# Differential attention with three slots of score banks and its map combination shared by VectorE and GpSimd

## The chip, the cores and the metric

The kernel runs on one core of one Trainium2 chip. The metric is the device time of one execution in microseconds. Engines are named as in the profile: PE is TensorE, DVE VectorE, ACT ScalarE, POOL GpSimd, SP SyncE. PSUM has eight banks of 512 float32 columns per partition; here all eight form one tensor `ps`.

## What is computed

A hybrid transformer of 2 layers on 512 tokens of width 1024, then a second block of 4 layers on the 512 latent tokens and 256 context tokens, with three kinds of mixers in turn. The change lies in the third layer of the second block, the only one of kind 2 (`mixer_c`), differential attention with 8 head pairs, each with two score maps of head width 64:

```python
def diff_attention(q, k, v, lam):
    scale = HEAD_DIM ** -0.5
    def block(j, qb):
        logits = jnp.einsum("bqhmd,bkhmd->bhmqk", qb, k).astype(jnp.float32) * scale
        p = jax.nn.softmax(logits, axis=-1)
        a = (p[:, :, 0] - lam * p[:, :, 1]).astype(v.dtype)
        return jnp.einsum("bhqk,bkhd->bqhd", a, v)
    return map_query_blocks(block, q)
...
o = finish(diff_attention(q, jnp.concatenate([kc, k], axis=1), jnp.concatenate([vc, v], axis=1), lam), s)
oc = finish(diff_attention(qc, kc, vc, lam), n_ctx) if need_ctx else None
```

Latent queries see all 768 keys, context queries the 256 context keys.

## The kernel before

The stage is the first one of `difference_attention` (lines 1283 to 1428). Its work is a list of 48 units in groups. A unit is one tile of 128 queries of one pair, with both of its maps. `second_block` makes the groups: first eight groups (one per pair) of four latent units, 768 keys each, then eight groups of two context units, 256 keys each. Queries and keys of a group are split into a high and a low float32r part; the next group's parts are made during a group by ACT (`q_high`, `k_high`) and POOL (`q_low_plain` L1117, `k_low` L1127).

Each engine runs its own loop over the units, in a fixed order with semaphores between them. For one unit:

- PE makes the scores of both maps (L1145), latent ones in four banks, two for each map; the next unit's scores go into the same four banks, so PE waits for both exponentials of this one (context units alternate between two pairs of banks).
- DVE takes each row's maximum of both maps from PSUM (L1407), ACT the exponentials with their row sums (L1362), a pair of instructions for each map; ring of three units in `prob`.
- DVE computes the reciprocals of the sums (L1397) and a weight per row (L1399), then combines both maps over all 768 columns in one instruction (L1419): map 1 times weight plus map 0.
- PE transposes the combined map two units later, six blocks (L1331), into banks 4 or 5 and bank 6; ACT copies the first four blocks to SBUF (L1370), DVE the other two, the tail (L1414). PE multiplies with the values three units later (L1343) into bank 7, ACT scales that into `prj` (L1354).
- Once per group, for the norm of the outputs: POOL clamps (L1306), ACT squares twice (L1386, L1389), DVE reduces to `near` and `far` (L1426).

A second stage (lines 1436 to 1493) scales the outputs. Two lines set what PE waits for before the scores:

```python
        return 2 * x - 2 if x and self.double(x) and self.double(x - 1) else 2 * x
...
                            pe.wait_ge(exped, max(1, W.exps_ahead(x)))
```

## Time and profile before

| | |
|---|---|
| three runs | 3370.6, 3384.76, 3385.7 us, median 3384.76 |
| the profiled execution | 3373.4 us, its span 3371.6 us |
| busy over the span | PE 3180.3 us (94%), DVE 1503.1 (45%), ACT 1340.1 (40%), POOL 1154.5 (34%) |
| mean granted TensorE clock | 0.98 |
| the stage of the change | from 2747.7 to 2931.3 us of the span |

Busy time is the time in which an engine has an instruction under way. The profiled execution's own time is what it reports as a run; its span is from its first to its last instruction. The other stages have no instruction that the change touches.

### The profile page before, as it was taken

How to read it: one execution, taken by the hardware profiler on the slowest of the kernel's cores; microseconds unless marked ns; L12 is line 12 of the kernel's file. 1: busy time of each engine (PE TensorE's matmuls, PEld its weight loads, DVE VectorE, ACT ScalarE, POOL GpSimd, SP SyncE). 2: the span in 40 equal slices, each digit the busy share in tenths (PEclk: the TensorE clock that was granted, in tenths of full speed). 3: DMA queues.
4: the chain of work that ended last, by engine and by line, in shares of the span. 5: the costliest groups of instructions: out<-in, count | busy, mean ns of one | idle time of the engine just before them, and what ended most of it. 6: DMA issues, size and time to landing. Idle time of an engine off the chain costs nothing. (4 is left out here: it accounts for less than half of the span.)

```text
span 3371.6 us, 52216 instructions
## 1 busy us (share of the span) xinstructions
PE 3180.3 (94%) x20854; PEld 2602.3 (77%) x20854; DVE 1503.1 (45%) x2671; ACT 1340.1 (40%) x2452; POOL 1154.5 (34%) x640
## 2 busy tenths in 40 slices
PE   7989999999989999989999999999999988799998
PEld 6857788877667888878787888777888767588787
DVE  4963444118744343131376310267323348833473
ACT  4353333223433333242366313267223237733463
POOL 4531444445314444434201322242234422226202
PEclk9999999999999999989999999999999999899999
DMA  4345222223452222222000111110112200013102
GB/s 148 114 158 187 82 100 94 98 84 120 157 192 77 100 94 97 100 91 88 26 2 18 56 60 63 55 44 15 57 62 88 76 19 1 4 54 103 48 2 76
DMA packets 81815, 262.19 MB, mean 78 GB/s; under 512 B 11936, under 2 KB 13344, under 8 KB 81568
## 3 DMA queue, kind: packets, MB, share of 16 engines
q1 hardware_dynamic: 81568, 258.79, 22.7%
q8 instruction: 169, 2.77, 0.3%
q14 instruction: 78, 0.64, 0.1%
HBM read 239.34 MB, written 2.10 MB: 72 GB/s over the span
## 5 line engine op out<-in xcount | busy, mean ns | idle before, releaser
L175 PE MATMUL ps<-hs,head 128*128 128x512 f32 x4176 | 868.3, 365 | 18.5 <-PEq L95 5.6
L175 PE MATMUL ps<-hs,WS 128*128 128x512 f32 x4176 | 861.3, 364 | 7.6 <-POOL WS L156 7.6
L175 PEld LDWEIGHTS ps<-hs,head 128*128 128x128 f32 x4176 | 713.0, 189 | 167.1 <-issue 19.1
L175 PEld LDWEIGHTS ps<-hs,WS 128*128 128x128 f32 x4176 | 713.3, 189 | 144.2 <-POOL WS L156 9.7
L156 POOL TENSOR_TENSOR WS<-W,WS 128x1024 fp32r<-128x1024 f32 x168 | 406.3, 2418 | 618.0 <-ACT WS L148 618.0
L156 POOL TENSOR_TENSOR head<-W,head 128x1024 fp32r<-128x1024 f32 x165 | 398.3, 2414 | 616.7 <-ACT head L148 616.5
L148 ACT CAST WS<-W 128x1024 fp32r<-128x1024 f32 x168 | 176.2, 1049 | 350.8 <-PE ps L175 324.2
L1630 ACT ACTIVATE prob<-ps,low 128x768 f32<-128x768 f32 (+4 forms) x320 | 223.4, 700 | 181.4 <-DVE low L1702 178.7
L1702 DVE TENSOR_REDUCE low<-ps 128x1 f32<-128x768 f32 (+4 forms) x320 | 216.5, 702 | 94.8 <-PE ps L1145 90.4
L148 ACT CAST head<-W 128x1024 fp32r<-128x1024 f32 x165 | 172.7, 1047 | 198.8 <-PE ps L175 198.6
L1145 PE MATMUL ps<-kk,qq 64*128 64x256 f32 (+3 forms) x2064 | 214.2, 334 | 38.3 <-ACT prob L1362 24.2
L1145 PEld LDWEIGHTS ps<-kk,qq 64*128 64x128 f32 x2064 | 158.0, 185 | 104.3 <-issue 50.7
L1117 POOL TENSOR_TENSOR qq<-prj,qq 128x512 fp32r<-128x512 f32 (+1 forms) x54 | 55.8, 1033 | 415.6 <-ACT qq L1110 406.0
L2072 DVE TENSOR_TENSOR glu<-cg,glu 128x512 fp32r<-128x512 f32 x44 | 81.0, 1840 | 258.1 <-ACT glu L2046 258.1
L1597 PE MATMUL ps<-const,prob 128*128 128x128 f32 x1312 | 182.9, 280 | 6.7 <-ACT probT L1638 3.3
L1612 PE MATMUL ps<-probT,vtok 128*64 128x128 f32 x2624 | 178.6, 279 | 2.4 <-DVE prj L1686 2.4
L1597 PEld LDWEIGHTS ps<-const,prob 128*128 128x128 f32 x1312 | 140.3, 141 | 38.4 <-ACT prob L1630 11.4
L2354 ACT ACTIVATE prj<-ps,par 128x768 f32<-128x768 f32 (+1 forms) x52 | 45.3, 871 | 306.1 <-PE ps L175 306.1
L1612 PEld LDWEIGHTS ps<-probT,vtok 128*64 128x64 f32 x2624 | 140.0, 136 | 27.6 <-issue 27.1
L1638 ACT COPY probT<-ps 128x512 f32<-128x512 f32 (+3 forms) x272 | 139.7, 541 | 1.7 <-PE ps L1597 1.4
L2104 DVE TENSOR_TENSOR xT<-xT,ps 128x512 f32<-128x512 f32 x32 | 22.0, 687 | 253.9 <-PE ps L175 253.9
L175 PE MATMUL ps<-head,hs 128*128 128x512 f32 (+2 forms) x624 | 120.4, 350 | 9.5 <-DVE hs L375 5.4
(290 smaller groups left out, 3925.4 us busy)
## 6 DMA issues: line engine op xcount, KB each, us to landing
W<-in_stream_dram SPq DMA_DIRECT2D x432, 512.0 KB, 3.5
swap<-prj SPq DMA_DIRECT2D x168, 64.0 KB, 2.1
band<-in_bias_band_dram SPq DMA_DIRECT2D x8, 512.0 KB, 3.5
prj<-prj SPq DMA_DIRECT2D x64, 64.0 KB, 2.9
xT<-in_x_dram SPq DMA_DIRECT2D x4, 512.0 KB, 8.3
W<-in_stream_dram SPq DMA_DIRECT2D x1, 2048.0 KB, 13.6
xT<-turned SPq DMA_DIRECT2D x8, 256.0 KB, 6.5
out_dram<-xT SPq DMA_DIRECT2D x8, 256.0 KB, 2.7
```

The costliest lines, as they stand in the source:

```text
L148: nc.scalar.copy(WS[j % 2][:, 0, :], M.W[:, (pos + j) % RING, :]).then_inc(high, 1)
L156: nc.gpsimd.tensor_tensor(WS[j % 2][:, 1, :], M.W[:, (pos + j) % RING, :], WS[j % 2][:, 0, :], ALU.subtract).then_inc(split, 1)
L175: last = pe.matmul(out, a(i), b(j), start=start and n == 0, stop=stop and n == 2)
L1117: return self.nc.gpsimd.tensor_tensor(self.q_part(s, 1, cols), self.queries(t, cols), self.q_part(s, 0, cols), ALU.subtract)
L1145: last = pe.matmul(out(hd)[:, sc:sc + c], self.qq[s][half(hd), i, q0:q0 + P], self.kk[s_keys][half(hd), j, kc:kc + c], start=n == 0, stop= ...
L1597: last = pe.transpose(turn_at(y, hd, j), prob[:, (2 * y + hd) % 4, sc:sc + P], M.const[:, C_ID:C_ID + P])
L1612: pe.matmul(summed_at(hd), M.vtok[:, kb, v_col(p) + 64 * hd:v_col(p) + 64 * hd + 64], probT[:, (2 * y + hd) % 4, j, :], start=j == 0, stop ...
L1630: nc.scalar.activation(prob[:, u % 4, c0:c0 + n], W.scores(M, x, hd)[:, c0:c0 + n], ACT.Exp, bias=low[:, u:u + 1], accum_out=total[:, u:u ...
L1638: nc.scalar.copy(probT[:, u % 4, 0:n, :], M.ps[:, 4 + 2 * hd, 0:n * P].rearrange("p (x n) -> p x n", n=P)).then_inc(turn_copied, 1)
L1702: nc.vector.tensor_reduce(low[:, u:u + 1], W.scores(M, x, hd)[:, c0:c0 + n], AX_X, ALU.max, negate=True).then_inc(maxed, 1)
L2072: nc.vector.tensor_tensor(glu[:, 1, f - 2, :], g[:, f % 2, :], glu[:, 0, f - 2, :], ALU.subtract).then_inc(glu_split, 1)
L2354: nc.scalar.activation(M.prj[:, t, 0:n], flat(bank(t), n), ACT.Copy, scale=gain(t)).then_inc(evicted, 1)
```

## The change

Score banks: the maps of all units go in turn through three slots of two banks (0 to 5), so the scores of unit x wait for the exponentials 0 to 2x-2, not for both of unit x-1. `prob` becomes a ring of four units. All transposes use bank 6, the first four blocks (the front) and then the last two (the back); they come three units after the scores, the product with the values four units after. DVE copies the front to SBUF, ACT the back. DVE combines the first 384 columns of a latent unit (all 256 of a context unit); POOL combines the last 384 in two instructions, a multiplication by the weight and an addition. DVE takes the maximum of map 1 after reciprocal, weight and front copy. A group is now one pair with four latent and two context units, so query and key parts are made eight times, for 768 queries, and clamp, squares and reductions are 768 wide. The scratch for dynamic DMAs is set to 1024 bytes, which frees SBUF.

```diff
@@ -1259,47 +1259,58 @@
...
-    ring, n_keys = 3, operands.n_keys
+    ring, n_keys, front = 4, operands.n_keys, 3 * P
...
-        clamped, scaled = sbuf(nc, mem, "clamped", [P, 2, S]), sbuf(nc, mem, "scaled", [P, S])
+        clamped, scaled = sbuf(nc, mem, "clamped", [P, 2, N]), sbuf(nc, mem, "scaled", [P, N])
...
-        turn_at = lambda x, j: (M.ps[:, 4 + x % 2, j * P:j * P + P] if j < 4 else M.ps[:, 6, (j - 4) * P:(j - 3) * P])
+        backs = lambda n: sum(not W.small(x) for x in range(n))
+        turns = lambda n: n + backs(n)
+        parts = lambda x: [W.columns(x)[i:i + 4] for i in range(0, W.size(x) // P, 4)]
+        turned_parts = lambda x, i: M.ps[:, 6, 0:len(parts(x)[i]) * P].rearrange("p (x n) -> p x n", n=P)
...
-        scores = lambda x, hd: W.scores(M, x, hd)[:, W.first(x):W.first(x) + W.size(x)]
...
+        def banks(x, hd):
+            b = 2 * ((2 * x + hd) % 3)
+            return M.ps[:, b:b + 2, :].rearrange("p b n -> p (b n)")
+
+        first = lambda x: 0 if W.small(x) else W.first(x)
+        scores = lambda x, hd: banks(x, hd)[:, first(x):first(x) + W.size(x)]
...
             @block.gpsimd
             def _(pool):
-                for y in range(X + 4):
+                for y in range(X + 3):
                     if y < X:
-                        g = works[y][0] + 1
-                        n, last = y - W.start[g - 1], len(groups[g - 1][3]) - 1
+                        pool.wait_ge(weight_known, y + 1)
+                        if not W.small(y):
+                            x = unit(y, 1)[:, front:]
+                            nc.gpsimd.tensor_tensor(x, x, weight[:, y:y + 1].broadcast_to([P, n_keys - front]), ALU.mult
+                                                    ).then_inc(back_weighted, 1)
+                            pool.wait_ge(back_weighted, backs(y + 1))
+                            nc.gpsimd.tensor_tensor(x, x, unit(y, 0)[:, front:], ALU.add).then_inc(back_combined, 1)
+                        g, n = works[y][0] + 1, y - W.start[works[y][0]]
                         if g < len(groups):
                             p, q_cols, k_cols, _ = groups[g]
-                            if n == min(1, last - 1):
+                            if n == 1:
                                 pool.wait_ge(queries_high, g)
-                                if y:
-                                    pool.wait_ge(weight_known, y)
                                 operands.q_low_plain(g % 2, p, q_cols).then_inc(queries_low, 1)
-                            if n == min(2, last - 1):
+                            if n == 2:
                                 pool.wait_ge(keys_high, g)
-                                if y:
-                                    pool.wait_ge(weight_known, y)
                                 operands.k_low(g % 2, p, k_cols).then_inc(keys_low, 1)
-                    if y - 3 in ends:
-                        g = ends.index(y - 3)
+                    if y - 2 in ends:
+                        g = ends.index(y - 2)
                         pool.wait_ge(raw_copied, ends[g])
                         if g >= 2:
                             pool.wait_ge(reduced, 2 * (g - 1))
@@ -1308,76 +1319,75 @@
 
             @block.tensor
-                for x in range(X + 3):
+                def turn(y, i):
+                    if y + i:
+                        pe.wait_ge(front_copied, y + i)
+                    if backs(y) and not i:
+                        pe.wait_ge(back_copied, backs(y))
+                    for j, sc in enumerate(parts(y)[i]):
+                        last = pe.transpose(M.ps[:, 6, j * P:j * P + P], prob[:, (2 * y + 1) % (2 * ring), sc:sc + P],
+                                            M.const[:, C_ID:C_ID + P])
+                    last.then_inc(turned, 1)
+
+                for x in range(X + 4):
...
                         if x:
-                            pe.wait_ge(exped, max(1, W.exps_ahead(x)))
-                        operands.scores(pe, lambda hd: W.scores(M, x, hd), g % 2, g % 2, m * P // 2, keys
-                                        ).then_inc(scored, 1)
+                            pe.wait_ge(exped, 2 * x - 1)
+                        operands.scores(pe, lambda hd: banks(x, hd), g % 2, g % 2, m * P // 2,
+                                        [(keys[0][0], 0, CTX)] if W.small(x) else keys).then_inc(scored, 1)
                         if x < 3:
                             keep_running(pe, M, 4, 7)
+                    if 3 <= x < X + 3:
+                        pe.wait_ge(front_combined, x - 2)
+                        if backs(x - 2):
+                            pe.wait_ge(back_combined, backs(x - 2))
+                        turn(x - 3, 0)
+                    if x >= 4:
+                        y = x - 4
-                        pe.wait_ge(turn_copied, y + 1)
-                        if W.tail(y):
-                            pe.wait_ge(tail_copied, tails(y + 1))
+                        pe.wait_ge(front_copied, y + 1)
+                        pe.wait_ge(back_copied, backs(y + 1))
...
+                    if 3 <= x < X + 3 and not W.small(x - 3):
+                        turn(x - 3, 1)
...
                             if x >= ring:
-                                act.wait_ge(turned, x - ring + 1)
+                                act.wait_ge(turned, turns(x - ring + 1))
                             nc.scalar.activation(unit(x, hd), scores(x, hd), ACT.Exp, bias=low[:, u:u + 1],
                                                  accum_out=total[:, u:u + 1]).then_inc(exped, 1)
-                    if 2 <= x < X + 2:
-                        y = x - 2
-                        n = min(4, W.size(y) // P)
-                        act.wait_ge(turned, y + 1)
-                        if y >= 2:
-                            act.wait_ge(weighted, y - 1)
-                        nc.scalar.copy(probT[:, y % 2, 0:n, :], M.ps[:, 4 + y % 2, 0:n * P].rearrange(
-                            "p (x n) -> p x n", n=P)).then_inc(turn_copied, 1)
+                    if 3 <= x < X + 3 and not W.small(x - 3):
+                        y = x - 3
+                        act.wait_ge(turned, turns(y + 1))
+                        nc.scalar.copy(probT[:, y % 2, 4:, :], turned_parts(y, 1)).then_inc(back_copied, 1)
...
             @block.vector
             def _(dve):
+                def largest(x, hd):
+                    u = 2 * x + hd
+                    nc.vector.tensor_reduce(low[:, u:u + 1], scores(x, hd), AX_X, ALU.max, negate=True
+                                            ).then_inc(maxed, 1)
+
                 for x in range(X + 8):
+                    if x < X:
+                        dve.wait_ge(scored, x + 1)
+                        largest(x, 0)
...
-                    for hd in range(2):
-                        if x < X:
-                            u = 2 * x + hd
-                            if hd == 0:
-                                dve.wait_ge(scored, x + 1)
-                            nc.vector.tensor_reduce(low[:, u:u + 1], scores(x, hd), AX_X, ALU.max, negate=True
-                                                    ).then_inc(maxed, 1)
-                    if 2 <= x < X + 2 and W.tail(x - 2):
-                        y = x - 2
-                        dve.wait_ge(turned, y + 1)
+                    if 3 <= x < X + 3:
+                        y = x - 3
+                        dve.wait_ge(turned, turns(y) + 1)
                         if y >= 2:
                             dve.wait_ge(weighted, y - 1)
-                        nc.vector.tensor_copy(probT[:, y % 2, 4:4 + W.tail(y), :], M.ps[:, 6, 0:W.tail(y) * P].rearrange(
-                            "p (x n) -> p x n", n=P)).then_inc(tail_copied, 1)
+                        nc.vector.tensor_copy(probT[:, y % 2, 0:len(parts(y)[0]), :], turned_parts(y, 0)
+                                              ).then_inc(front_copied, 1)
+                    if x < X:
+                        largest(x, 1)
                     if 1 <= x <= X:
                         y = x - 1
+                        n = CTX if W.small(y) else front
                         dve.wait_ge(weight_known, y + 1)
-                        nc.vector.scalar_tensor_tensor(unit(y, 1), unit(y, 1), weight[:, y:y + 1], unit(y, 0), ALU.mult,
-                                                       ALU.add).then_inc(combined, 1)
+                        nc.vector.scalar_tensor_tensor(unit(y, 1)[:, 0:n], unit(y, 1)[:, 0:n], weight[:, y:y + 1],
+                                                       unit(y, 0)[:, 0:n], ALU.mult, ALU.add).then_inc(front_combined, 1)
...
@@ -2509,14 +2523,17 @@
                     tiles = ([(2 * m + 1, ((m * P, 0, NEAR), context_keys), (0, 0, NEAR)) for m in range(QT - 1)] +
                              [("edges", ((0, 0, P), (S - P, P, P), context_keys), (0, 0, NEAR))])
                 groups = [(p, (0, S), (0, N), tiles) for p in range(PAIRS2)]
-                if go_on:
+                if kind == 2:
+                    tiles += [context(m) for m in range(QT, NT)]
+                    groups = [(p, (0, N), (0, N), tiles) for p in range(PAIRS2)]
+                elif go_on:
                     groups += [(p, (S, N), (S, N), [context(m) for m in range(QT, NT)]) for p in range(PAIRS2)]
...
-                    first_rows(nc, M, FirstRows(operands, (0, S), (0, N)))
+                    first_rows(nc, M, FirstRows(operands, groups[0][1], (0, N)))
...
-    nc = bacc.Bacc("TRN2", target_bir_lowering=False, num_devices=1)
+    nc = bacc.Bacc("TRN2", target_bir_lowering=False, num_devices=1, dynamic_dma_scratch_size=1024)
```

DVE in the steady part of the latent units, all rows of one unit, before:

```order
L1399 SCALAR_TENSOR_TENSOR weight<-inv,small,total 128x1
L1407 TENSOR_REDUCE low<-ps 128x1 x2
L1414 COPY probT<-ps 128x256
L1419 SCALAR_TENSOR_TENSOR prob<-prob,weight 128x768
L1397 RECIPROCAL inv<-total 128x2
```

and with the change:

```order
L1405 TENSOR_REDUCE low<-ps 128x1
L1415 RECIPROCAL inv<-total 128x2
L1417 SCALAR_TENSOR_TENSOR weight<-inv,small,total 128x1
L1425 COPY probT<-ps 128x512
L1405 TENSOR_REDUCE low<-ps 128x1
L1433 SCALAR_TENSOR_TENSOR prob<-prob,weight 128x384
```

The second maximum moved behind the weight and the copy from PSUM, which is now the front of 512 columns, and the combine is half as wide.

POOL in one group of the change, from its second latent unit (`prob` is the pair of maps, `qq` and `kk` are the low parts of the next group, `clamped` the outputs of the last one):

```order
L1299 TENSOR_TENSOR prob<-prob,weight 128x384
L1302 TENSOR_TENSOR prob<-prob 128x384
L1117 TENSOR_TENSOR qq<-prj,qq 128x768
L1299 TENSOR_TENSOR prob<-prob,weight 128x384
L1302 TENSOR_TENSOR prob<-prob 128x384
L1127 TENSOR_TENSOR kk<-prj,kk 128x768
L1317 TENSOR_SCALAR clamped<-prj 128x768
L1299 TENSOR_TENSOR prob<-prob,weight 128x384
L1302 TENSOR_TENSOR prob<-prob 128x384
```

Before, POOL had in this stage three rows a group, L1117, L1127 and L1306. Two rows per latent unit were added ahead of them.

PE for one latent unit, before:

```order
L1145 MATMUL ps<-kk,qq 128x512 x6
L1145 MATMUL ps<-kk,qq 128x256 x6
L1331 MATMUL ps<-const,prob 128x128 x6
L1343 MATMUL ps<-vtok,probT 128x128 x6
```

and with the change:

```order
L1145 MATMUL ps<-kk,qq 128x512 x6
L1145 MATMUL ps<-kk,qq 128x256 x6
L1328 MATMUL ps<-const,prob 128x128 x4
L1357 MATMUL ps<-vtok,probT 128x128 x6
L1328 MATMUL ps<-const,prob 128x128 x2
```

The last two transposes moved behind the product and stand ahead of the next unit's scores.

## Rows read from the trace of the kernel before

**Rows 1.** Timeline, the marks: start us, length us, engine, operation [idle before]
```profile
2747.76 1.31 PE L1145 MATMUL ps<-kk,qq 64*128 64x512 f32 x12 [1.74 <-PEq L95]
...
2885.53 0.62 PE L1145 MATMUL ps<-kk,qq 64*128 64x256 f32 x6 [1.03 <-ACT prob L1362]
...
2920.77 0.61 PE L1145 MATMUL ps<-kk,qq 64*128 64x256 f32 x6
...
2930.93 0.41 DVE L1426 TENSOR_REDUCE far<-scaled 128x2 f32<-128x256 f32 x1
```

**Rows 2.** Stretches: us; PE, PEld, DVE, ACT, POOL busy; clock, DMA
```profile
2747.70:2885.50 137.80, 112.21 (x936) 96.33 (x937) 113.89 (x198) 98.37 (x215) 27.45 (x23) 1.00 0.00 1
...
2899.00:2925.00 26.00, 20.54 (x132) 15.32 (x132) 21.52 (x67) 23.37 (x89) 9.75 (x16) 0.87 0.00 1
```

**Rows 3.** Timeline, one latent unit on PE, DVE and ACT
```profile
2769.26 1.31 PE L1145 MATMUL ps<-kk,qq 64*128 64x512 f32 x12 [0.82 <-ACT prob L1362]
...
2770.50 0.64 PEld L1331 LDWEIGHTS ps<-const,prob 128*128 128x128 f32 x6
...
2770.62 1.82 DVE L1407 TENSOR_REDUCE low<-ps 128x1 f32<-128x768 f32 x2 [0.88 <-PE ps L1145]
2771.11 1.42 PEld L1343 LDWEIGHTS ps<-vtok,probT 128*128 128x128 f32 x12
...
2771.62 0.90 ACT L1362 ACTIVATE prob<-ps,low 128x768 f32<-128x768 f32 x1 [1.66 <-DVE low L1407]
2772.36 0.42 DVE L1414 COPY probT<-ps 128x256 f32<-128x256 f32 x1
...
2772.51 0.89 ACT L1362 ACTIVATE prob<-ps,low 128x768 f32<-128x768 f32 x1
2772.69 1.01 DVE L1419 SCALAR_TENSOR_TENSOR prob<-prob,weight 128x768 f32<-128x768 f32 x1
...
2773.54 1.33 PE L1145 MATMUL ps<-kk,qq 64*128 64x512 f32 x12 [0.82 <-ACT prob L1362]
2773.62 0.16 DVE L1397 RECIPROCAL inv<-total 128x2 f32<-128x2 f32 x1
2773.81 0.22 DVE L1399 SCALAR_TENSOR_TENSOR weight<-inv,small,total 128x1 f32<-128x1 f32 x1
```

**Rows 4.** Groups by line and form: count | busy us, mean ns | idle before
```profile
L1718 DVE COPY probT<-ps 128x512 f32<-128x512 f32 x64 | 43.6, 681 | 4.6 <-PE ps L1597 4.6
...
L1407 DVE TENSOR_REDUCE low<-ps 128x1 f32<-128x256 f32 x32 | 12.1, 419 | 4.5 <-PE ps L1145 4.2
...
L1419 DVE SCALAR_TENSOR_TENSOR prob<-prob,weight 128x256 f32<-128x256 f32 x16 | 8.1, 509 | 0.0
...
L1127 POOL TENSOR_TENSOR kk<-prj,kk 128x768 fp32r<-128x768 f32 x20 | 36.4, 1821 | 54.5 <-ACT kk L1124 39.9 <-DVEq L92 14.6
...
L1306 POOL TENSOR_SCALAR clamped<-prj 128x512 f32<-128x512 f32 x8 | 5.2, 646 | 0.7
...
L1005 POOL TENSOR_TENSOR k_far<-k_far,prj 128x384 f32<-128x384 f32 x2 | 2.0, 998 | 0.0
L981 POOL TENSOR_TENSOR q_far<-prj 128x384 f32<-128x384 f32 x2 | 1.7, 870 | 0.0
```

**Rows 5.** Timeline, three places where DVE and POOL work at once
```profile
390.98 2.40 POOL L156 TENSOR_TENSOR head<-W,head 128x1024 fp32r<-128x1024 f32 x1 [3.48 <-ACT head L148]
391.97 1.95 DVE L2072 TENSOR_TENSOR glu<-cg,glu 128x512 fp32r<-128x512 f32 x1 [8.12 <-ACT glu L2046]
...
2779.06 1.81 POOL L1127 TENSOR_TENSOR kk<-prj,kk 128x768 fp32r<-128x768 f32 x1 [3.21 <-ACT kk L1124]
...
2779.20 1.82 DVE L1407 TENSOR_REDUCE low<-ps 128x1 f32<-128x768 f32 x2 [0.88 <-PE ps L1145]
...
2881.86 0.74 POOL L1127 TENSOR_TENSOR kk<-prj,kk 128x256 fp32r<-128x256 f32 x1 [3.53 <-DVE near L1426]
2881.91 0.69 DVE L1399 SCALAR_TENSOR_TENSOR weight<-inv,small,total 128x1 f32<-128x1 f32 x1
```

More of the change, by code:

```diff
@@ L1261, in difference_attention @@
     X, works, groups = W.X, W.works, W.groups
-    tails = lambda n: sum(W.tail(x) > 0 for x in range(n))
     ends = W.start[1:]
-    ring, n_keys = 3, operands.n_keys
+    ring, n_keys, front = 4, operands.n_keys, 3 * P
     width = lambda g: len(groups[g][3]) * P
@@ L1349, in _ @@
                 for x in range(X + 6):
-                    if 4 <= x < X + 4:
-                        p, m = works[x - 4][1:3]
-                        act.wait_ge(weighted, x - 3)
-                        act.wait_ge(inverted, x - 3)
-                        nc.scalar.activation(M.prj[:, p, m * P // 2:m * P // 2 + P], summed, ACT.Copy,
-                                             scale=inv[:, 2 * (x - 4):2 * (x - 4) + 1]).then_inc(raw_copied, 1)
                     if x < X:
```

36 lines of the change are left out of this document (14 added, 22 removed).

## The prediction

> **What bounds the kernel now.** The page comes first: over the whole span PE is busy 94% of the time, so most of this kernel is matmul and is not touched. The change lies in one stage, so that stage is cut out of the trace. Its first scores start at 2747.76, the first context unit's at 2885.53, the last unit's at 2920.77, and its last reduction ends at 2931.34, 183.6 us after the start [rows 1]. So 32 latent units take 137.8 us (4.31 each) and 15 steps of context units 35.2 us (2.35 each); one pair costs 4 x 4.31 + 2 x 2.35 = 21.9 us. In the latent stretch no engine is full: DVE 114 of 138 us, PE 112, ACT 98, POOL 27 [rows 2]. What sets the period is a loop, and one unit in order of time shows it [rows 3]: the scores start at 2769.26; DVE gets them after 1.36 us and takes two row maxima; the first exponential starts 1.00 later, the second 0.89 after that, it is done 1.03 later, and the next scores start at 2773.54. That is 4.28. PE waited 0.81 us for ACT. DVE's own work in it, from start to start, is 1.74 (two maxima) + 0.33 (tail copy) + 0.93 (combine) + 0.33 (reciprocal and weight) = 3.33 us.
>
> **What the change does to that loop.** With three score slots, scores of unit x+1 need only the first exponential of unit x, so the second maximum and the second exponential leave the loop: 1.36 + 1.00 + 1.03 = 3.4 us would be left. But the loop is then no longer the limit; the queues of DVE and POOL are. I walked the 48 units through the new order of the four engines rules: an instruction starts when its engine is free and 0.05 us after what it waits for, and it holds its engine for the start-to-start time of the rows. On PE these are 1.24 for latent scores, 0.11 per transposed block and 1.42 for a product of six blocks; on ACT 0.88 per exponential [rows 3]. A pair is four latent units a to d and two context units e and f.
>
> DVE's own work for a pair, by start-to-start times: maxima 4 x 1.74 + 2 x 0.68 = 8.32 (a 256-column one takes 0.42 [rows 4], of which 0.08 overlaps the next, as with the long ones); reciprocals and weights 6 x 0.33 = 1.98; front copies from PSUM, 4 of 512 columns and 2 of 256, 4 x 0.61 + 2 x 0.33 = 3.10 (0.68 and 0.42 long [rows 3, 4]); combines: 768 columns take 1.01 and 256 take 0.51, so 384 take 0.61, and 4 x 0.53 + 2 x 0.40 = 2.92; near and far, now 768 columns, 2 x 0.87 = 1.74 (as a maximum of that width). Sum 18.1. The old order's DVE work for the same six units was nearly the same (4 x 3.33 + 2 x 1.41, and near and far of 1.9, so 18.0): halving the combine saves 4 x 0.40, the longer front copy gives back 4 x 0.28, and the context units' copies, which were ACT's, come on top.
>
> POOL's work rises steeply. An in-place two-input operation of 384 columns takes 1.00, one with a repeated column 0.87 [rows 4]: 1.87 per latent unit, 0.05 between them for the semaphore, plus per pair two 768-column low parts of 1.82 and a clamp (0.65 at 512 columns, so 0.9). Some 12 us per pair, below DVE's; as a queue it has room.
>
> **Does POOL's work lie beside DVE's for nothing? The trace says no.** A DVE product with two SBUF inputs, 512 columns, starts at 391.97 while POOL runs from 390.98 to 393.38. It ends at 393.92, which is 0.54 after POOL's end: it stood still until then [rows 5]. A one-column weight instruction, 0.22 long elsewhere [rows 3], starts at 2881.91, 0.05 after POOL's k_low, and takes 0.69, to POOL's end at 2882.60 [rows 5]. Two maxima, which read PSUM, take 1.82 beside a POOL operation and 1.82 without one [rows 3, 5]. So combine and weight are held by a POOL operation under way, maxima are not, and copies from PSUM I take to be like maxima, since both read one input and that from PSUM. The Trainium skill says in "SBUF — State Buffer", section "Who interferes with whom", that a VectorE instruction with at most one SBUF input does not contend; by this the trace's maxima agree, and the front copies would be free as I take them.
>
> The holds in the walk (microseconds from a's first maximum): weight of a at 5.01; POOL multiplies from 5.28 to 6.14 and adds from 6.19 to 7.19. DVE meanwhile copies and takes the second maximum and is at the combine of a at 6.35: held to 7.19, then 0.40 of columns, a loss of 0.71. Unit b repeats it, 0.71. POOL then does q_low until 13.86, so the weight of c (DVE there at 13.16) loses 0.56, and its combine 0.35. k_low until 17.98 holds the weight of d 1.09, clamp and multiplication its combine 0.68, the addition of d the weight of e 0.28. Together 4.4 us. DVE waits 1.0 more for scores, where PE sits behind the front copy. A pair: 18.1 + 4.4 + 1.0 = **23.4 us against 21.9**.
>
> No row shows the two POOL operations themselves. Bounds: 0.62 each from below (one input over 512 columns takes 0.65 [rows 4]), 1.25 from above (the 1.00 with half a further input for the weight). The walk gives 22.4 and 24.6 us a pair at these ends. I take the rows of the same width. As the holds come from few examples, their ends are nothing (rival A) and the full 4.4.
>
> The Trainium skill, "GPSIMD Engine Reference", section "4.1 Engine selection", sends elementwise multiplications to VectorE, with GpSimd about 2 times slower for two inputs. By that rule each half-width operation would be 2 x 0.61 = 1.2 us, an estimate from the page; the walk would come to 24.3 us a pair, and the stage would be 7 us longer still.
>
> **The sum.** Walk: first two pairs 21.7 and 22.1 (the pipe fills, nothing behind the first scores), five pairs at 23.4, the last up to its sixth scores 19.6: 180.4. The drain is longer than before: it is one unit deeper, and clamp, two squares and two reductions of the last pair are 768 wide in a row: 15.0 instead of 10.6. Stage 195.4. The same walk over the old order gives 180.6 where the trace has 183.6, so I scale by 1.016: 198.5, **+14.9**. Ahead of it the first high part of the queries (ACT) grows by 256 columns, and its low part (DVE) now ends beside POOL's k_low: +0.3, at about 1 ns a column as in the combine. On PE all work stays, and its share of the time falls. It had the full 2.4 GHz (granted 1.00) in the latent stretch and 0.87 of it on average among context units, where PE was waiting more [rows 2]; I add 1 us. Total +16. DMAs: none added; all are issued by SP, so the smaller scratch costs nothing, and no DMA runs in this stage (share 0.00 [rows 2]) that could be late.
>
> Against the profiled execution's own 3373.4 (span 3371.6) that is 3389. The median of the three runs, 3384.8, stands 11 above the profiled one, and against it I forecast **3401**. A measurement of this kernel tells from no change about 0.5%, 17 us; the forecast lies just at that line.
>
> **The rivals.**
> A, the holds are absorbed. In the walk with no hold DVE waits 3.3 us per pair for scores, PE being behind copies: the pair is 21.35 and the stage 184.4, scaled. Holds of 4.4 that fell wholly into such waits or that turned round (DVE first at the port, POOL waiting, which has room) would leave this. For: POOL's slack; the margins at a and b are only 0.16 us. Against: weight and combine stand in DVE's own queue before the next maximum. Decided by whether the combine reaches the port before the addition. It gives +1: 3386, not slower.
> B, real overlap: the extra score slot keeps DVE fed, neither holds nor waits bind, and a pair costs little over DVE's 18.1, say 19.4; with the longer drain that is 20 us less, 3365. Against: PE is in order, and the second turn stands ahead of the next scores, behind the front copy. It decides if the front copy is done before PE has finished its products.
> C, the clock. PE's own work by the walk's times is 15.6 of 23.4 us per pair. If the granted clock stays near 0.87 [rows 2], that work grows by 2.3 us per pair, at worst all on the path, 18 us; the walk with PE's operations 15% longer gives 6 us more. So 3407, at most 3419. For: context units now come every pair, and PE waits up to 2 us there. Against: 0.87 came only after a run of small units.
>
> **How the numbers follow.** Forecast (3393 to 3411) 0.50, A 0.22, B 0.10, C 0.18. Faster by over 0.5% (under 3368) is B and the rim of A: 0.12. Slower by over 0.5% (over 3401.7) is C and half of the forecast: 0.45. The rest, 0.43, is within. The range takes in the bounds of the POOL prices (22.4 to 24.6 per pair: -8 and +10), A, and the lower half of C: 3374 to 3416.
>
> **What would show it.** In the changed profile: L1405 of 768 columns starts again 23.4 us later from pair to pair; L1433 of 384 columns with a mean near 1.1 rather than 0.61; L1417 with single ones of 0.5 to 1.2; L1299 and L1302 at 0.86 and 1.00; L1405's wait for PE small, because DVE is nearly full. Wrong if L1433 stays near 0.6 (A), if pairs take 20 us (B), if the clock of the stage is under 0.95 (C), or if L1425 is held by POOL too, which the walk leaves out.

## The result, and the profile after

The changed kernel takes 3404.31 us (median of 5 runs, 3400.48 to 3408.2), the kernel before 3380.59 (5 runs, 3370.6 to 3385.7): a ratio of 1.007, 95% interval 1.0054 to 1.0085. That is 23.7 us slower. The forecast was 3401 with a range of 3374 to 3416, so the time is met. Its closeness is partly luck: I had added 16 us to a median of 3384.76, the fuller median is 4 lower, and on the old one the same +23.7 would have given 3408.5, still inside the range but 7.5 over the forecast instead of 3.3. The 8 us missing from my +16 are the lesson of this case.

The page of the kernel after, its first lines:

```profile
span 3402.5 us, 52186 instructions
...
PE 3202.4 (94%) x20854; PEld 2617.9 (77%) x20854; DVE 1522.2 (45%) x2671; ACT 1329.2 (39%) x2404; POOL 1211.8 (36%) x680
```

The marks of the stage in its timeline, answering to [rows 1] (start us, length us, engine, operation):

```profile
2754.49 1.31 PE L1145 MATMUL ps<-kk,qq 64*128 64x512 f32 x12 [2.00 <-PEq L95]
...
2947.01 0.64 PE L1145 MATMUL ps<-kk,qq 64*128 64x256 f32 x6
...
2961.41 0.94 DVE L1440 TENSOR_REDUCE far<-scaled 128x6 f32<-128x768 f32 x1
```

From first scores to last reduction the stage takes 207.9 us against 183.6: +24.3, the whole difference of the medians. Behind it both traces take the same (440.15 and 440.26 us). Ahead of it this one is 6.7 later, but that start lies between 2743.7 and 2758.8 over all the profiles below, whatever the edit, so 6.4 of it is scatter; the wider first rows are the 0.3 forecast (query high part 0.84 instead of 0.63).

Stretches after, answering to [rows 2]: the whole stage, then the second pair and three of the steady ones (us; PE, PEld, DVE, ACT, POOL busy; clock, DMA):

```profile
2754.49:2962.35 207.86, 163.57 (x1176) 134.08 (x1176) 167.65 (x304) 126.11 (x303) 97.56 (x86) 0.89 0.00 1
...
2778.67:2801.08 22.41, 17.68 (x145) 14.24 (x144) 19.48 (x37) 13.91 (x37) 12.88 (x11) 1.00 0.01 1
...
2801.08:2826.29 25.21, 21.16 (x145) 17.41 (x145) 21.55 (x39) 15.89 (x39) 12.70 (x11) 0.80 0.00 1
...
2826.29:2851.16 24.87, 20.26 (x145) 16.94 (x144) 20.91 (x39) 15.78 (x39) 12.71 (x11) 0.86 0.00 1
...
2851.16:2875.41 24.25, 18.73 (x145) 15.48 (x144) 21.29 (x39) 15.75 (x39) 12.71 (x11) 0.93 0.00 1
```

Two things stand there. A steady pair takes 24.25 to 25.6 us, the walk gave 23.4. And the clock is not the 1.00 of the old latent stretch: it was 0.97 over the stage before and is 0.89 now. Only the second pair runs at 1.00, and it takes 22.4, where the walk gave 22.1.

Groups of the stage by line and form, answering to [rows 4] (count | busy us, mean ns | idle before), and from the view of single lines the spread of each (ns min/median/max):

```profile
L1405 DVE TENSOR_REDUCE low<-ps 128x1 f32<-128x768 f32 x64 | 60.6, 949 | 20.0 <-PE ps L1145 20.0
...
L1433 DVE SCALAR_TENSOR_TENSOR prob<-prob,weight 128x384 f32<-128x384 f32 x32 | 32.2, 1006 | 0.0
...
L1405 DVE TENSOR_REDUCE low<-ps 128x1 f32<-128x256 f32 x32 | 13.3, 416 | 13.6 <-PE ps L1145 13.6
```

```profile
L1433 DVE SCALAR_TENSOR_TENSOR prob<-prob,weight x48: 470/610/1392, 2762.7 to 2951.7; 128x384 f32<-128x384 f32 x32, 128x256 f32<-128x256 f32 x16
...
L1417 DVE SCALAR_TENSOR_TENSOR weight<-inv,small,total x48: 219/220/1247, 2761.7 to 2950.2; 128x1 f32<-128x1 f32 x48
...
L1425 DVE COPY probT<-ps x48: 417/678/693, 2769.3 to 2955.2; 128x512 f32<-128x512 f32 x32, 128x256 f32<-128x256 f32 x16
...
L1299 POOL TENSOR_TENSOR prob<-prob,weight x32: 825/826/1197, 2762.0 to 2944.4; 128x384 f32<-128x384 f32 x32
...
L1302 POOL TENSOR_TENSOR prob<-prob x32: 992/1009/1327, 2762.9 to 2945.3; 128x384 f32<-128x384 f32 x32
```

The combine of 384 columns takes 1.01 us in the mean where an unheld one takes 0.61, a weight up to 1.25 where it needs 0.22, and the copy from PSUM is never held. POOL's two operations take 0.83 and 1.01 in the median (0.89 and 1.05 in the mean, as some are held themselves), the prices taken from rows of the same width. DVE waits 33.6 us for scores, in a stage where I had called it nearly full.

How a hold looks, and what the clock does, in the timeline of the third pair (start us, length us):

```profile
2818.24 2.13 POOL L1127 TENSOR_TENSOR kk<-prj,kk 128x768 fp32r<-128x768 f32 x1
...
2819.16 1.23 DVE L1417 SCALAR_TENSOR_TENSOR weight<-inv,small,total 128x1 f32<-128x1 f32 x1
...
2820.07 2.77 PE L1357 MATMUL ps<-vtok,probT 128*128 128x128 f32 x12
...
2821.26 0.61 DVE L1433 SCALAR_TENSOR_TENSOR prob<-prob,weight 128x384 f32<-128x384 f32 x1
2821.36 1.20 POOL L1299 TENSOR_TENSOR prob<-prob,weight 128x384 f32<-128x384 f32 x1
...
2824.25 0.42 DVE L1405 TENSOR_REDUCE low<-ps 128x1 f32<-128x256 f32 x1 [2.38 <-PE ps L1145]
...
2824.64 1.50 PE L1357 MATMUL ps<-vtok,probT 128*128 128x128 f32 x12
...
2833.93 1.02 POOL L1302 TENSOR_TENSOR prob<-prob 128x384 f32<-128x384 f32 x1
2833.97 1.39 DVE L1433 SCALAR_TENSOR_TENSOR prob<-prob,weight 128x384 f32<-128x384 f32 x1
```

The one-column weight starts at 2819.16 and ends at 2820.39, with POOL's low part (2820.37). The combine of 2833.97, 0.04 behind POOL's addition, ends 0.41 after it. At 2821.26 the combine comes first: it takes its 0.61, and POOL's multiplication is the one held (1.20 instead of 0.83). And the product at 2820.07 takes 2.77 us where the next, at 2824.64, takes 1.50 for the same matmuls: half the clock for most of it, and DVE then waits 2.38 us for the scores queued behind it.

### The profile page after: what moved, and what is told of

It reads as the page before. It is cut to its first block and busy times, and to the rows that moved or that the text cites. A ratio compares the mean times of both kernels' runs of the same rounds, so it can differ in the third digit from the quotient of the medians.

```text
span 3402.5 us, 52186 instructions
## 1 busy us (share of the span) xinstructions
PE 3202.4 (94%) x20854; PEld 2617.9 (77%) x20854; DVE 1522.2 (45%) x2671; ACT 1329.2 (39%) x2404; POOL 1211.8 (36%) x680
## 3 DMA queue, kind: packets, MB, share of 16 engines
q8 instruction: 169, 2.77, 0.3%
## 5 line engine op out<-in xcount | busy, mean ns | idle before, releaser
L175 PEld LDWEIGHTS ps<-hs,head 128*128 128x128 f32 x4176 | 715.5, 190 | 165.8 <-issue 19.4
L175 PEld LDWEIGHTS ps<-hs,WS 128*128 128x128 f32 x4176 | 712.9, 189 | 144.6 <-POOL WS L156 10.5
L1644 ACT ACTIVATE prob<-ps,low 128x768 f32<-128x768 f32 (+4 forms) x320 | 223.2, 699 | 183.4 <-DVE low L1716 180.8
L1117 POOL TENSOR_TENSOR qq<-prj,qq 128x512 fp32r<-128x512 f32 (+2 forms) x46 | 55.5, 1207 | 311.4 <-ACT qq L1110 310.9
## 6 DMA issues: line engine op xcount, KB each, us to landing
W<-in_stream_dram SPq DMA_DIRECT2D x1, 2048.0 KB, 13.6
```

Source lines behind the costliest of these rows:

```text
L175: last = pe.matmul(out, a(i), b(j), start=start and n == 0, stop=stop and n == 2)
L1117: return self.nc.gpsimd.tensor_tensor(self.q_part(s, 1, cols), self.queries(t, cols), self.q_part(s, 0, cols), ALU.subtract)
L1644: nc.scalar.activation(prob[:, u % 4, c0:c0 + n], W.scores(M, x, hd)[:, c0:c0 + n], ACT.Exp, bias=low[:, u:u + 1], accum_out=total[:, u:u ...
```

## The experiments

All are measured against the kernel before on the same chip (3376.0, 3378.3 and 3377.8 us in the three sets). The first number of each is its median, and the ratio is the one on record with its interval. The ratio is not the quotient of the two medians and differs from it by up to 0.2%, or 6 us. A stage is read from one profile each.

### The scratch alone, and the grouping alone

```diff
-    nc = bacc.Bacc("TRN2", target_bir_lowering=False, num_devices=1)
+    nc = bacc.Bacc("TRN2", target_bir_lowering=False, num_devices=1, dynamic_dma_scratch_size=1024)
```

> The kernel before with only the scratch for dynamic DMAs set to 1024 bytes. In the changed kernel's profile the stage starts 6.7 us later in the span than before, though only 0.3 of that was expected from the wider first rows. Theory that this is scatter between executions, as the three runs before differ by 15 us: no difference, ratio 1.000 within 0.002. Rival, the smaller scratch slows the weight stream: about +6 us, ratio 1.002.

3375.3 us, ratio 0.9994 (0.9983 to 1.0004), stage 183.4: the scratch costs nothing, and it can be kept in the others.

The kernel before with the scratch and with groups of four latent and two context units (768-wide `clamped` and `scaled` with them), nothing else:

```diff
-                if go_on:
+                if kind == 2:
+                    tiles += [context(m) for m in range(QT, NT)]
+                    groups = [(p, (0, N), (0, N), tiles) for p in range(PAIRS2)]
+                elif go_on:
```

> The kernel before with the change's groups (one pair, four latent and two context units; 768-wide parts, clamp, squares, reductions) and its scratch, nothing else. By the walk, a context unit inside a group costs 2.6 us instead of 2.3 on average, and the last drain is wider: stage 191 against 183.6, +8 us, if the clock stays as before. If units of both kinds side by side lower TensorE's clock: +12 to +20. Rival, the grouping only saves work (half as many low and high parts) and the loss is all from POOL and the slots: -2 to 0 us.

3391.5 us, ratio 1.0042 (1.0028 to 1.0055), +14 by the ratio, with the old slots and no new work on POOL. The stage takes 194.6, +11. Two of its pairs, the third and the seventh, the same instructions in each:

```profile
2804.10:2826.58 22.48, 16.79 (x146) 14.24 (x145) 18.50 (x36) 16.61 (x41) 4.45 (x3) 1.00 0.00 1
...
2895.40:2918.65 23.25, 18.34 (x145) 15.57 (x144) 18.50 (x36) 16.61 (x41) 4.45 (x3) 0.93 0.00 1
```

Latent steps are 4.28 as before. A context step is 2.69 or 2.70 each time, where a long run of context units had pipelined to 2.35: 16 of them make 5.4 us. The clock falls to 0.93 in five of the first seven pairs (never in the old latent stretch [rows 2]), with six single latent steps of 4.5 to 5.25, 4.0 us together over the usual 4.28. The drain behind the last unit's scores takes 13.3 us instead of 10.6. Grouping is thus dear by itself.

The other way round, the changed kernel with the groups of before (and the places of the high and low parts that go with them):

> The changed kernel with the groups of before (eight of four latent units, then eight of two context units); slots, order and the shared combination stay. Walk with POOL holding DVE: stage 199, as slow as the changed one, with 4.6 us per latent unit, since low parts still come every fourth unit. If the grouping (and the clock it costs) is what made it slow and the holds cost little: stage about 185 or less, +2 us over before.

3399.2 us, ratio 1.0059 (1.0038 to 1.008), stage 205.45, 6 over the walk's 199: almost nothing came back. The profile shows a wait that the old grouping brings with it (timeline ahead of the fifth group's first scores):

```profile
2820.31 0.83 POOL L1299 TENSOR_TENSOR prob<-prob,weight 128x384 f32<-128x384 f32 x1 [1.04 <-DVE weight L1421]
...
2821.22 0.99 POOL L1302 TENSOR_TENSOR prob<-prob 128x384 f32<-128x384 f32 x1
...
2822.17 2.12 POOL L1127 TENSOR_TENSOR kk<-prj,kk 128x768 fp32r<-128x768 f32 x1
...
2824.39 1.04 PE L1145 MATMUL ps<-kk,qq 64*128 64x512 f32 x6 [3.06 <-issue]
```

With four units a group the key low part is the last thing before the next group's scores, and it now stands behind multiplication and addition: every fourth step is 6.8 us, and PE stands still for 3. The profile names no releaser for that idle time ("issue"), but the scores start 0.10 us after the low part's end. The two context units in the new groups had covered that. So groups and POOL's queue are coupled, and undoing either alone shows little. The clock falls here with the old groups too: it is 0.93 over the latent units, where the kernel before had 1.00.

### What POOL's half costs

The changed kernel, DVE combining all 768 columns:

```diff
-    ring, n_keys, front = 4, operands.n_keys, 3 * P
+    ring, n_keys, front = 4, operands.n_keys, 6 * P
...
-                        if not W.small(y):
-                            x = unit(y, 1)[:, front:]
...
```

> The changed kernel with the whole combination on DVE (one instruction of 768 columns, 1.0 us) and none on POOL. DVE's own work per pair rises by 4 x 0.4 = 1.6 us, the holds by multiplication and addition (about 3 of 4.4 us) go. Walk: 22.7 to 23.1 us per pair, stage 193 to 198 before any loss of clock, so 2 to 5 us faster than the changed kernel. If DVE's load is the limit and holds are nothing: 3 x 1.6 to 8 x 1.6 us, 5 to 13 slower than the changed kernel. If only the clock matters: the same as the changed kernel.

3392.9 us, ratio 1.0031 (1.0018 to 1.0043), stage 202.4: 16.9 us over the kernel before by the medians and 10.5 by the ratio, where the whole change has 23.7, and 5.4 less in the stage: faster than with POOL's help. DVE does twice the columns and yet loses nothing by it, its combine taking 1.26 us for 768 columns (some still held by low parts) against 1.01 held for 384. Of the 5.4 us, 4.2 lie in the steps from the first to the second context unit, four of which take 3.99 us here and only one as little in the changed kernel; the section on the clock explains these.

POOL's two instructions left out, DVE keeping 384 columns (the last 384 stay uncombined):

> The changed kernel in which the last 384 columns of each latent unit's combination are left out: POOL does neither multiplication nor addition, those columns keep map 1's exponentials. DVE's work is unchanged. Theory of the holds: combines come back to 0.61 us but for those behind low parts and clamp; walk 22.0 us per pair or less, stage 186 to 194 against 207.9 in the changed kernel's profile, so 14 to 20 us faster than the changed kernel. Rival, the loss is the clock and PE's order: at most 3 us faster.

3391.6 us, ratio 1.0032 (1.0019 to 1.0044), stage 193.7, 14.2 less than the changed kernel. The combine still takes 0.86 us in the mean, since low parts now fall beside it. And in their place two memsets of nearly the same length on POOL, into a buffer of their own, with the same semaphores:

```diff
-                            x = unit(y, 1)[:, front:]
-                            nc.gpsimd.tensor_tensor(x, x, weight[:, y:y + 1].broadcast_to([P, n_keys - front]), ALU.mult
-                                                    ).then_inc(back_weighted, 1)
+                            if backs(y):
+                                pool.wait_ge(back_combined, backs(y))
+                            nc.gpsimd.memset(idle[:, 0:864], 0.0).then_inc(back_weighted, 1)
...
-                            nc.gpsimd.tensor_tensor(x, x, unit(y, 0)[:, front:], ALU.add).then_inc(back_combined, 1)
+                            nc.gpsimd.memset(idle[:, 0:1024], 0.0).then_inc(back_combined, 1)
```

> As the kernel with the last 384 columns left out, but POOL writes zeros to a buffer of its own (864 and 1024 columns of bfloat16) in place of multiplication and addition, with the same semaphores: POOL is as busy in its queue and PE waits for it, but it reads nothing. Theory that the loss is VectorE held while POOL reads SBUF: no holds, within 4 us of the kernel with the columns left out, combines of 0.61 us. Rival, the loss is that PE waits for a slow POOL queue: as slow as the changed kernel. If any POOL instruction holds DVE, also writes: combines of 1.0 us and as slow as the changed kernel.

3389.4 us, ratio 1.0039 (1.0023 to 1.0055). Its groups in the stage:

```profile
L1303 POOL MEMSET idle<- 128x1024 bf16 x32 | 30.4, 951 | 1.9
L1301 POOL MEMSET idle<- 128x864 bf16 x32 | 26.2, 817 | 88.9 <-DVE weight L1418 87.9
L1434 DVE SCALAR_TENSOR_TENSOR prob<-prob,weight 128x384 f32<-128x384 f32 x32 | 19.4, 607 | 0.0
L1418 DVE SCALAR_TENSOR_TENSOR weight<-inv,small,total 128x1 f32<-128x1 f32 x48 | 17.4, 362 | 1.7
```

POOL is nearly as long busy (88 us of the stage, 98 with the real work), it stands as long between weight and transposes, its memsets do write SBUF, and yet the combine takes 0.607 each time and the stage 194.9. So not the queue and not the writing costs the 13 us, but that POOL reads. (2.1 of the 13 lie in the steps from the first to the second context unit, where the clock falls less often.) The Trainium skill says in "SBUF — State Buffer", section "Who interferes with whom", that a VectorE instruction with two SBUF inputs contends with a GpSimd instruction that reads SBUF and not with one that only writes; these two runs agree (1.01 beside reading operations, 0.61 beside memsets). The weight's 0.36 is that of units held by operations which still read, the low parts above all (0.5 and 0.95 us).

### The clock

In the run without POOL's half the same pair appears at both clocks:

```profile
2821.41:2843.21 21.80, 17.48 (x146) 14.19 (x146) 19.10 (x39) 15.74 (x39) 4.46 (x3) 1.00 0.00 1
2843.21:2866.45 23.24, 18.91 (x145) 15.63 (x145) 19.05 (x38) 15.76 (x39) 4.46 (x3) 0.93 0.00 1
```

and its timeline shows where, transposes and product in the step of the first context unit, first at full clock, then not:

```profile
2838.35 0.63 PE L1322 MATMUL ps<-const,prob 128*128 128x128 f32 x4 [1.25 <-ACT probT L1369]
2838.82 1.50 PE L1349 MATMUL ps<-vtok,probT 128*128 128x128 f32 x12
...
2860.16 1.09 PE L1322 MATMUL ps<-const,prob 128*128 128x128 f32 x4 [1.25 <-ACT probT L1369]
2861.04 2.53 PE L1349 MATMUL ps<-vtok,probT 128*128 128x128 f32 x12
```

The step grows from 3.99 to 5.43 us, the pair from 21.80 to 23.24, by the same 1.44. One fall of the clock there costs 1.4 us, wholly on the path, since DVE and ACT wait for the scores behind that product. Both times PE had been idle 1.22, 1.05 and 1.25 us in turn just ahead, so these gaps alone don't decide whether the clock falls.

I then tried to hold the clock with idle transposes in the changed kernel:

```diff
+                    if 3 <= x < X and x - W.start[works[x][0]] in (2, 3, 4, 5):
+                        pe.wait_ge(exped, 2 * x)
+                        for _ in range(4):
+                            pe.matmul(M.ps[:, 2 * ((2 * x + 2) % 3), 0:P], M.const[:, C_ID:C_ID + P], M.const[:, 0:P],
+                                      start=True, stop=True)
```

> The changed kernel with four idle transposes of 128 columns (0.42 us at the full clock) on PE ahead of the back's transposes, in the last four steps of each pair, where PE waits for copies anyway; they write to the score bank that is free next. Nothing else of it changes. The stage's mean granted clock is 0.89 in the changed kernel against 0.97 before, and its step from e to f takes 5.2 to 5.9 us where the walk has 4.1. Theory that the 9 us over the forecast stage are the clock: the clock rises to 0.95 or more, the stage falls by 4 to 9 us. Rival, the long step is order, not clock: the stage grows by up to 32 x 0.42 = 13 us, or stays.

3410.6 us, ratio 1.0096 (1.0076 to 1.0115), stage 212.1, 4.2 longer where the theory had it 4 to 9 shorter. Two stretches of one pair's length, each from the scores of a second context unit to those of the next:

```profile
2799.05:2823.84 24.79, 21.05 (x178) 17.77 (x177) 21.28 (x38) 15.85 (x38) 12.69 (x12) 1.00 0.01 2
2823.84:2850.25 26.41, 22.69 (x177) 19.41 (x177) 21.28 (x38) 15.86 (x38) 13.99 (x13) 0.94 0.00 1
```

The clock rose (0.97 over the stage) and the step fell from 5.2 to 5.9 down to 4.88 in five pairs of eight, but the fillers (32.8 us of PE in all) put the time back: 24.79 for a pair at full clock, as much as an unfilled one at 0.86. As a remedy it fails: the stage grew, as the rival had it, though the clock rose. As a test it agrees that the long step is the clock (4.88 at 1.00, 6.3 to 6.5 in the three pairs where the clock fell all the same) and says nothing cleaner on its size, as the fillers also add a wait of PE for two exponentials.

### The order of the queues

The changed kernel with the old groups, POOL's low parts ahead of its half, and reciprocal and weight behind both maxima:

```diff
                             if n == min(1, last - 1):
                                 pool.wait_ge(queries_high, g)
+                                if y:
+                                    pool.wait_ge(weight_known, y)
...
+                        pool.wait_ge(weight_known, y + 1)
+                        if not W.small(y):
+                            x = unit(y, 1)[:, front:]
...
```

> The changed kernel with three things put differently: the groups of before; POOL makes the low parts ahead of multiplication and addition (the next group's scores waited 6.8 us every fourth unit for the keys' low part in the run with the old groups); DVE computes reciprocal and weight after both maxima, so that the combine follows the weight at once and starts before POOL's multiplication. Theory of the holds: the walk gives 174 to 179, scaled 177 to 182, 2 to 7 us faster than before. If holds were not the cause and the three slots themselves lose: as slow as the run with the old groups, 20 us over before.

3376.1 us, ratio 0.9993 (0.9982 to 1.0005), stage 182.2. The wait of the low part is gone, but POOL's half still costs: combine 1.14, multiplication 0.92, addition 1.15 us in the mean. The combine does start ahead of POOL's multiplication, as intended, and in 25 of 32 latent units it is held all the same. Two units in the timeline:

```profile
2814.80 1.28 DVE L1441 SCALAR_TENSOR_TENSOR prob<-prob,weight 128x384 f32<-128x384 f32 x1
2814.85 0.83 POOL L1313 TENSOR_TENSOR prob<-prob,weight 128x384 f32<-128x384 f32 x1 [0.64 <-DVE weight L1434]
...
2823.94 0.62 DVE L1441 SCALAR_TENSOR_TENSOR prob<-prob,weight 128x384 f32<-128x384 f32 x1
2823.99 1.25 POOL L1313 TENSOR_TENSOR prob<-prob,weight 128x384 f32<-128x384 f32 x1 [1.78 <-DVE weight L1434]
```

In the first the combine is held, in the second the multiplication is. Unrounded, the 25 held combines start 0.043 or 0.044 us ahead, and the seven free ones 0.048 or 0.049. The same with the combine on DVE alone:

> The same with the whole combination on DVE, none on POOL. Walk 173 to 177, scaled 176 to 180: 4 to 8 us faster than before, and as fast as the one shared with POOL or faster. If DVE's load were the limit: 0.4 x 32 = 13 us slower than the shared one.

3366.2 us, ratio 0.9968 (0.9953 to 0.9982): 12 us faster than the kernel before by the medians, 11 by the ratio, the best of the study. Its stage (the view of stretches), and two groups of it:

```profile
2748.61:2921.65 173.04, 145.24 (x1176) 119.81 (x1176) 162.52 (x320) 129.73 (x335) 41.36 (x46) 0.99 0.01 1
```

```profile
L1433 DVE SCALAR_TENSOR_TENSOR prob<-prob,weight 128x768 f32<-128x768 f32 x32 | 32.6, 1019 | 1.1
...
L1426 DVE SCALAR_TENSOR_TENSOR weight<-inv,small,total 128x1 f32<-128x1 f32 x48 | 12.1, 253 | 1.7
```

Almost nothing is held (1.02 and 0.25; a few weights of context units take up to 0.77), the clock stays at 0.99, and latent steps take 3.76, 3.93, 4.21 and 4.12 instead of 4.28. DVE is busy 94% of the stage: this is what the three slots give with the new order of the queues, 10.5 us, until DVE is full.

With reciprocal and weight back between the two maxima, and nothing else changed:

> The reordered kernel with the combination on DVE, but reciprocal and weight back where the change has them, after the first maximum. Tells what of its gain comes from the place of the weight. DVE, waiting there for the second exponential of the last unit, which is behind that unit's second maximum, should lose time in every latent unit: the walk gives 191 against 173, so some 15 us slower than the reordered one, 4 slower than before. If the place does not matter: the same as the reordered one.

3390.0 us, ratio 1.0039 (1.0025 to 1.0053), stage 192.5, 19.4 longer for two instructions moved. The weights, in the view of their line:

```profile
L1417 DVE SCALAR_TENSOR_TENSOR weight<-inv,small,total x48: 219/221/1801, 2757.0 to 2936.0; 128x1 f32<-128x1 f32 x48
```

In its timeline a query low part and a weight start together:

```profile
2812.37 1.28 POOL L1117 TENSOR_TENSOR qq<-prj,qq 128x512 fp32r<-128x512 f32 x1 [7.83 <-ACT qq L1110]
```

```profile
2812.36 1.30 DVE L1417 SCALAR_TENSOR_TENSOR weight<-inv,small,total 128x1 f32<-128x1 f32 x1
```

The weight ends with POOL's operation, at 2813.66 and 2813.65. In the mean it takes 0.554 us against 0.253 behind both maxima, so 48 x 0.30 = 14.4 us of the 19.4. The expected time was met for another reason than the expected one: DVE never waits there for an exponential, it is the weight itself that is held.

Two splits of the transposes in the best kernel, three and three blocks, and two and four, instead of four and two:

```diff
-        parts = lambda x: [W.columns(x)[i:i + 4] for i in range(0, W.size(x) // P, 4)]
+        parts = lambda x: [W.columns(x)] if W.small(x) else [W.columns(x)[:3], W.columns(x)[3:]]
```

> The reordered kernel with the combination on DVE, with the six transposed blocks parted three and three instead of four and two: DVE's copy falls from 0.68 to about 0.55, ACT's grows from 0.36 to 0.46. Walk: stage 2.7 us shorter, so 170 to 173 where the trace of the reordered one has 173.0. If DVE were not the limit there: no difference.

> The same with two blocks on DVE and four on ACT: copies of 0.42 and 0.58. Walk: 3.0 us shorter than four and two, 15 us under before in all. If ACT's longer copy delays the next exponential: no better than three and three, or worse.

3370.0 us each, ratios 0.9975 (0.9962 to 0.9988) and 0.9974 (0.9962 to 0.9986). The stages, 171.7 and 172.0, are about 1 us shorter than 173.0, which the run times don't show. Shifting columns from DVE to ACT has little left to give.

## Why the prediction was right, and where not

**The loop and the queues: right.** With three slots the score loop no longer binds; the first two steps of a pair are 3.68 and 3.65 (walk 3.63 and 3.7). DVE's own 18.1 us per pair is met: over the seven pairs from the second (2776.60 to 2949.00) its holds are 28 combines x (1.048 - 0.610) and 43 weights x (0.426 - 0.220), together 21.2, so 3.0 a pair; its waits are 25.2 for scores and 0.9 for transposes, so 3.7 a pair; 18.1 + 3.0 + 3.7 = 24.8, and the pairs take 24.6.

**The holds: right in kind, smaller in size.** 3.0 us a pair instead of 4.4. The walk had the unit c's weight and d's combine behind POOL for 0.56 and 0.68; in the trace c's weight loses 0.50 in four of these seven pairs and nothing in three, and d's combine comes first and loses nothing. Rival A has its point there, that the order can turn round, but only in one unit of four, and at a, with 0.04 us between them, POOL was first. They are absorbed in part only: with memsets the holds are 16.5 us less (12.8 of combines, 3.7 of weights) and the stage is 13.0 shorter, 2.1 of it by the clock. Rival A is excluded by L1433's mean of 1.01, rival B by pairs of 24 to 26, and the copies from PSUM are indeed free.

**POOL's prices: right.** 0.83 and 1.01 in the median against 0.86 and 1.00 taken. The Trainium skill's factor of 2 ("GPSIMD Engine Reference", "4.1 Engine selection") had stood for an estimate of 1.2 each and 24.3 us a pair. The pairs are about that long, but not for that reason: the trace has 1.36 and 1.66 times DVE's 0.61.

**The term that failed: the clock, "I add 1 us".** I had argued that 0.87 came only after a run of small units and took rival C's condition for the exception. It is the rule: the clock falls in seven of eight pairs, in the step from the first to the second context unit. By the starts of scores these steps are 5.23, 4.08, 5.63, 5.61, 5.29, 5.88, 5.44 and 5.56 us; the 4.08 is the one at clock 1.00, like the walk's 4.1 and the 3.99 without POOL's half. The excess over 4.05 is 10.3 us. The walk's stage of 198.5 plus 10.3 is 208.8, and the trace has 207.9. So rival C's mechanism came on top of the forecast's, at the size that I had given it (6 to 18 more); by my own sign, a clock of the stage under 0.95, the forecast was wrong in this term. The time stayed within its own 3393 to 3411 because these bounds leave 10 us above the forecast, and the median that came out 4 us lower helped. That 208.8 and 207.9 agree doesn't prove each term: the holds came out 1.4 us a pair under the walk's, and DVE's waits for scores 2.6 over its 1.0, of which the clock explains about 1.3. So two errors of about the same size cancel.

**"L1405's wait for PE small": wrong.** It is 33.6 us. Of it 13.6 lie ahead of the maxima of f, the second context unit, largely behind the slow products (1.4 to 2.4 us a pair, and 0.23 in the pair at clock 1.00). Another 9.1 lie ahead of a's maxima, 1.3 a pair, which the walk had at about that size, and 8.4 while the pipe fills, ahead of the first four units.

**What makes the clock fall stays open.** The grouping alone brings falls (0.93 in five pairs of seven, against 1.00 before), though in latent steps there and not between the context units; and the old groups in the changed kernel don't take them away (0.93 over the latent units), while the reordered kernels with old groups have 0.99 and 1.00 there. That the wide gaps of PE are what brings the falls is argued from the rows only, and the two pairs without POOL's half, with the same three gaps and different clocks, show that it can't be these alone.

**Sums on the side.** Rival B's price doesn't follow from its own terms: seven pairs at 19.4, a last one about 3.8 shorter and a drain of 15.0 make 166.4, or 169 scaled, which is 14 or 15 us under the 183.6 and not 20. The chance of "slower by over 0.5%" by its own terms is 0.43 and not 0.45. Neither changes the forecast.

**Where the gain of the slots went.** Three parts that don't simply add: the new groups (+11 in the stage when alone), POOL's reads (+13 within the change), and the weight's place beside POOL's low part (+19 within the best kernel). With none of them, the slots give -10.5. Not run was the best kernel with either of low part order or old groups taken back alone, so their shares in it stay open, as does a clean figure for the clock, which no run here could hold at 1.00 without cost.

## What to carry to other kernels

Before POOL takes over work of DVE, look which of DVE's two-input SBUF instructions its reads will fall beside: here moving half of a 1.02 us combine to POOL left DVE with 1.01 us, and the kernel was slower than with all of it on DVE. Where a helper must read, place DVE's small two-input instructions away from it; a 0.22 us instruction took up to 1.8. And when a reordering puts short units among long ones, price the clock in each repetition, from a row at the lower level, rather than once for the stage.

## What the hardware showed that I had not expected

- The hold lasts exactly to POOL's end, and the columns follow: 0.41 us after it for 384 columns, 0.02 for one. A one-column instruction is as dear as a wide one.
- The order of the two starts decides, but by the recorded starts the tie isn't at zero: POOL 0.04 ahead holds DVE for 0.78 us; DVE 0.10 ahead holds POOL for 0.37; and DVE 0.043 or 0.044 ahead is held all the same (25 combines of the reordered kernel), while from 0.048 on it is not (seven).
- POOL's own operations grow too: low parts that start 0.45 us before the end of a held combine take 2.12 or 2.13 us, two that start beside none 1.80 and 1.85. So a hold makes the next one longer.
- Memsets of 0.82 and 0.95 us on POOL, which write SBUF without reading, don't hold the combine at all (607 ns, 32 times).
